# Block products with seven multiplications for the up projection of three chunk pairs

## The reference, cut to what matters

```python
D_MODEL = 1024
SEQ = 1024
DEPTH = 2
D_FF = 4 * D_MODEL
for l in range(DEPTH):
    ...
    x = layer_norm(DEEPNORM_ALPHA * x + jnp.einsum('btm,md->btd', mix, w_out[l]), ln_g[l, 0], ln_b[l, 0])
    hid = jnp.square(jax.nn.relu(jnp.einsum('btd,df->btf', x, w_up[l])))
    x = layer_norm(DEEPNORM_ALPHA * x + jnp.einsum('btf,fd->btd', hid, w_down[l]), ln_g[l, 1], ln_b[l, 1])
```

## Time and profile before

| | |
|---|---|
| time, median of 3 runs | 2765.5 us |
| span of the profiled execution | 2765.6 us |
| instructions | 36226 |
| PE busy | 2688.9 us, 12768 matmuls |
| DVE busy | 1645.8 us, 3330 |
| ACT busy | 998.6 us, 2055 |
| POOL busy | 1262.5 us, 1170 |
| DMA | 203.21 MB, mean 73 GB/s |
| mean granted TensorE clock | 0.990 |

### The profile page before, as it was taken

One profiled execution on the slowest core, in us unless ns is written; L12 is line 12 of the kernel. 1 busy time (PEld: TensorE's weight loads), 2 busy tenths in 40 slices (PEclk: granted clock), 3 DMA queues, 4 the chain that ended last, 5 costly groups with the idle time before them and its releaser, 6 DMA issues.

```text
span 2765.6 us, 36226 instructions
## 1 busy us (share of the span) xinstructions
PE 2688.9 (97%) x12768; PEld 2102.4 (76%) x12768; DVE 1645.8 (60%) x3330; ACT 998.6 (36%) x2055; POOL 1262.5 (46%) x1170
## 2 busy tenths in 40 slices
PE   8999899999999999999999998999999999999997
PEld 7788467668788888888887875676787888888886
DVE  3787876635534355544959877776364534355448
ACT  2476454442222212222435654443422222212223
POOL 5433700014666556666364346001156566566661
PEclk9999899999999999999999999999999999999999
DMA  5311344523311111101152122355323101111102
GB/s 155 89 46 46 68 91 93 131 105 97 122 33 32 61 62 61 50 17 63 65 138 57 44 74 57 79 109 119 114 89 111 57 27 39 61 62 61 50 20 80
DMA packets 97418, 203.21 MB, mean 73 GB/s; under 512 B 14010, under 2 KB 23162, under 8 KB 96954
## 3 DMA queue, kind: packets, MB, share of 16 engines
q1 hardware_dynamic: 87800, 175.58, 23.5%
q10 hardware_dynamic: 9440, 25.33, 2.5%
HBM read 138.04 MB, written 8.61 MB: 53 GB/s over the span
## 4 chain that ended last, share of the span: by engine, by line
PE 87%; DVE 7%; issue 2%; DMA 2%; ACT 1%; SPq 1%; POOL 0%; ACTq 0%; DVEq 0%; POOLq 0%
PE ps L1276 8%; PE ps L1278 8%; PE ps L1277 8%; PE ps L1158 8%; PE ps L1301 7%; PE ps L1300 7%; PE ps L1302 7%; PE ps L942 4%; PE ps L943 4%; PE ps L944 4%; PE ps L1206 2%; PE ps L1208 2%; PE ps L1207 2%; PE ps L1133 1%; PE ps L1100 1%
## 5 line engine op out<-in xcount | busy, mean ns | idle before, releaser
L900 POOL TENSOR_TENSOR wlo<-wraw,whi 128x512 fp32r<-128x512 f32 (+2 forms) x336 | 444.7, 1324 | 202.1 <-ACT whi L1363 180.2
L898 POOL CAST whi<-wraw 128x512 fp32r<-128x512 f32 (+2 forms) x272 | 183.6, 675 | 740.2 <-DMA wraw<-in_w_out 289.4
L1276 PE MATMUL ps<-xhi,whi 128*128 128x512 f32 x1024 | 406.1, 397 | 0.0
L1278 PE MATMUL ps<-xhi,wlo 128*128 128x512 f32 x1024 | 405.9, 396 | 0.0
L1277 PE MATMUL ps<-xlo,whi 128*128 128x512 f32 x1024 | 405.9, 396 | 0.0
L2064 DVE TENSOR_TENSOR common<-common,ps 128x512 f32<-128x512 f32 x104 | 69.6, 687 | 460.4 <-PE ps L1302 459.9
L1301 PE MATMUL ps<-wlo,op_hi 128*128 128x512 f32 x784 | 311.7, 398 | 0.0
L1300 PE MATMUL ps<-whi,op_hi 128*128 128x512 f32 x784 | 309.5, 395 | 0.0
L1302 PE MATMUL ps<-whi,op_lo 128*128 128x512 f32 x784 | 308.0, 393 | 0.0
L1507 ACT ACTIVATE probT<-ps 128x512 f32<-128x512 f32 (+2 forms) x456 | 205.2, 457 | 240.4 <-PE ps L1142 73.8
L900 POOL TENSOR_TENSOR wlo<-down_raw,whi 128x512 fp32r<-128x512 f32 x168 | 226.2, 1349 | 98.7 <-ACT whi L1363 92.0
(11 more groups left out here) (249 smaller groups left out, 5495.4 us busy)
## 6 DMA issues: line engine op xcount, KB each, us to landing
wraw<-in_w_up SPq DMA_DIRECT2D x144, 256.0 KB, 3.1
down_raw<-in_w_down SPq DMA_DIRECT2D x112, 256.0 KB, 3.6
wraw<-in_w_in SPq DMA_DIRECT2D x80, 256.0 KB, 2.7
slot<-q_part SPq DMA_DIRECT2D x72, 256.0 KB
slot<-k_part SPq DMA_DIRECT2D x72, 256.0 KB
wraw<-in_w_out SPq DMA_DIRECT2D x64, 256.0 KB, 2.8
slot<-q_part SPq DMA_DIRECT2D x48, 128.0 KB
slot<-k_part SPq DMA_DIRECT2D x48, 128.0 KB
```

The lines of the kernel that those rows point to most:

```text
L900: nc.gpsimd.tensor_tensor(lo, loaded, hi.bitcast(F32), ALU.subtract).then_inc(S["w_lo"], 1)
L1276: mm(ps[:, b, :], wh, xhi[:, k, tok], start=(k == 0), stop=False)
L1278: last = mm(ps[:, b, :], wl, xhi[:, k, tok], start=False, stop=(k == KT - 1))
```

## The change: three chunk pairs with seven products each

Chunks 0 and 1 are computed as before. Chunks 2 and 3, 4 and 5, 6 and 7 become pairs g = 1, 2, 3. For a pair, a 1024 x 1024 block of w_up stands against the 1024 x 1024 matrix x, both cut into quarters, and the same seven-product scheme is used (UPS names the weight side, UP_X the side of x). Each product has 4 slabs of 12 matmuls. Raw quarters of w_up lie in four "blocks" of four slabs; POOL forms S1 to S4 in place (line 1197 of the new kernel), right behind the lo part of a slab. The sums T1 to T4 of x are made once per layer while up(1) runs: POOL adds hi and lo of x back together (`whole`), DVE subtracts and makes lo parts, ACT makes hi parts, SyncE writes them to DRAM (x_sums, 8 MB per layer). In every pair they are loaded again, 1 MB at a time, into the three places that the operands of the down products use too. PSUM banks are drained by ACT copies and DVE additions (`add_product`).

The down products of two chunks now stand side by side and accumulate in the same banks, so that DVE adds 28 banks per pair instead of 28 per chunk; DOWNS gives (0,1), (2,3), (4,5) and (6). All hi parts of the slabs of pairs and of products are written by ACT. Semaphores that both layers can share are shared.

```diff
+DOWNS = [(0, 1), (2, 3), (4, 5), (6,)]
+N_DOWNS = len(DOWNS)
+PAIRS = range(1, N_DOWNS)
+UPS = ("A11", "A12", "S2", "S1", "S3", "S4", "A22")
+UP_X = ((0, 0), (4, 0), "T2", "T1", "T3", (4, 1), "T4")
+UP_BANK = (4, 0, 4, 0, 4, 0, 4)
+UP_FRESH = (0, 1, 3)
+X_SUMS = ("T1", "T3", "T2", "T4")
...
+def entries(g):
+    return [(q, c) for q in range(N_PROD) for c in DOWNS[g]]
...
+    for g in range(N_DOWNS):
+        if g:
+            for j, name in enumerate(UP_X):
+                if isinstance(name, str):
+                    for half in range(2):
+                        yield "x", g, (j, half)
+        for q, c in entries(g):
+            yield "operand", c, q
...
-    for c in range(FF_CHUNKS):
-        if c < LAST:
-            for k in range(KT):
-                yield "up", k, c + 1
-            for q in range(N_PROD):
-                for i in range(2):
-                    yield "product", i, (c, q)
+    for k in range(KT):
+        yield "up", k, 1
+    for g in range(N_DOWNS):
+        if g:
+            for j in range(len(UPS)):
+                for k in range(4):
+                    yield "pair", k, (g, j)
+        for q, c in entries(g):
+            for i in range(2):
+                yield "product", i, (c, q)
...
-    n for n, z in enumerate(SLABS) if z[0] == "product" and z[2][1] >= 4] + list(range(SLAB_LAST, N_SLABS))
+    n for n, z in enumerate(SLABS) if z[0] in ("product", "pair") or n in UP_SPLIT] + list(range(SLAB_LAST, N_SLABS))
...
+def sums_after(n):
+    kind, k, z = SLABS[n]
+    if kind == "up" and z == 1 and k >= 4:
+        return [("T3" if k % 2 == 0 else "T1", 0, (k - 4) // 2)]
+    if kind == "pair":
+        g, j = z
+        return {0: [("S1", g, k)], 1: [("S3", g, k)] + [("S2", g, 0)] * (k == 3), 2: [("S2", g, k + 1)] * (k < 3),
+                3: [("S4", g, k)], 4: [("T3" if k < 2 else "T1", DOWNS[g][0], k % 2)]}.get(j, [])
+    if kind == "product":
+        c, q = z
+        g = [c in cs for cs in DOWNS].index(True)
+        if len(DOWNS[g]) == 1:
+            return {1: [("T2", c, k)], 2: [("T4", c, k)]}.get(q, [])
+        odd = DOWNS[g][1]
+        if c != odd:
+            return {0: [("T2", c, k)], 1: [("T3", odd, k)], 2: [("T4", c, k)], 3: [("T4", odd, k)]}.get(q, [])
+        return {1: [("T1", c, k)], 2: [("T2", c, k)]}.get(q, [])
+    return []
...
+RECON_AFTER = {SLAB_UP0 + KT + 5: (0, 0), SLAB_UP0 + KT + 6: (0, 1), SLAB_UP0 + KT + 7: (1, 0), slab_up(1): (1, 1),
+               slab_up(1) + 3: (2, 0), slab_up(1) + 4: (2, 1), slab_up(1) + 5: (3, 0), slab_up(1) + 6: (3, 1)}
...
+                for g in PAIRS:
+                    split_done(slab_product(DOWNS[g - 1][-1], N_PROD - 1) + 1)
+                    load_block_of(g, "A21")
+                    load_block_of(g, "first A22")
+                    for k in range(8):
+                        load_down(DOWNS[g][0], k)
+                    load_x(g, t2, 0)
+                    load_x(g, t2, 1)
+                    load_x(g, t1, 0)
+                    load_x(g, t1, 1)
+                    load_x(g, t3_, 0)
+                    split_done(slab_pair(g, t2) + 3)
+                    sp.wait_ge(S["a_sum"], passed(l, "a_sum") + sum_count(("S4", g, 3)))
+                    load_block_of(g, "A22")
+                    more = g + 1 < N_DOWNS
+                    if more:
+                        split_done(slab_pair(g, UPS.index("S1")) + 3)
+                        load_block_of(g + 1, "A11")
+                    load_x(g, t3_, 1)
+                    load_x(g, t4, 0)
+                    if more:
+                        split_done(slab_pair(g, UPS.index("S3")) + 3)
+                        load_block_of(g + 1, "A12")
+                    load_x(g, t4, 1)
+                    split_done(slab_pair(g, UPS.index("S4")) + 3)
+                    if more:
+                        load_block_of(g, "low odd")
+                        split_done(slab_pair(g, UPS.index("A22")) + 3)
+                        load_block_of(g, "high odd")
...
+                nc.gpsimd.tensor_tensor(dst, a, b, op).then_inc(S["a_sum"], 1)
+                pool.wait_ge(S["a_sum"], passed(l, "a_sum") + sum_count(key))
...
+                for j in range(2 * half, 2 * half + 2):
+                    k_tile, tok = ((k, 0), (k, W), (4 + k, W), (4 + k, 0))[j]
+                    hi, lo = (z[:, k_tile, tok:tok + W].bitcast(F32) for z in (xhi, xlo))
+                    nc.gpsimd.tensor_tensor(xt[k % 2][j][:], hi, lo, ALU.add).then_inc(S["x_whole"], 1)
...
+                if n in RECON_AFTER:
+                    whole(*RECON_AFTER[n])
+                if sums_after(n):
                     pool.wait_ge(S["w_lo"], n + 1)
-                    t_sum(z[0], "T2" if z[1] == 1 else "T4", k)
+                for key in sums_after(n):
+                    difference(key)
...
+            def up_pair(g):
+                for j in range(len(UPS)):
+                    for k in range(4):
+                        n = slab_pair(g, j) + k
+                        z = ring(l, n)
+                        pe.wait_ge(S["w_lo"], n + 1)
+                        if isinstance(UP_X[j], str):
+                            place = place_of("x", g, (j, k // 2))
+                            if k % 2 == 0:
+                                pe.wait_ge(place_loaded[place], 16 * (l * X_LOADS[place] + x_loads(g, j, k // 2)))
+                            x_hi, x_lo = (part[place][:, k % 2] for part in (op_hi, op_lo))
+                        else:
+                            k_tile, half = UP_X[j]
+                            x_hi, x_lo = (part[:, k_tile + k, W * half:W * half + W] for part in (xhi, xlo))
+                        more = j not in UP_FRESH
+                        for f in range(4):
+                            if k == 0:
+                                up_bank_free(g, j, f)
+                            o = ps[:, UP_BANK[j] + f, :]
+                            wh, wl = whi[z][:, P * f:P * f + P], wlo[z][:, P * f:P * f + P]
+                            mm(o, wh, x_hi, start=(k == 0 and not more), stop=False, skip_group_check=more)
+                            mm(o, wh, x_lo, start=False, stop=False, skip_group_check=more)
+                            last = mm(o, wl, x_hi, start=False, stop=(k == 3), skip_group_check=more)
+                            if k == 3:
+                                last.then_inc(S["u_ready"], 1)
+                        if k < 3:
+                            last.then_inc(S["w_used"], 1)
...
+                    for c in cs:
+                        for i in range(2):
+                            n = slab_product(c, q) + i
+                            j = ring(l, n)
...
+            def x_differences(k):
+                t, low, high = xt[k % 2], xt_low[k % 2], xt_high[k % 2]
+                dve.wait_ge(S["x_whole"], passed(l, "x_whole") + 4 * k + 4)
+                for j, (a, b) in enumerate(((1, 0), (2, 1), (2, 0), (3, 2))):
+                    v_.tensor_tensor(t[j][:], t[a][:], t[b][:], ALU.subtract).then_inc(S["xt_sum"], 1)
+                    dve.wait_ge(S["xt_sum"], passed(l, "xt_sum") + 4 * k + j + 1)
+                for j in range(4):
+                    dve.wait_ge(S["xt_hi"], passed(l, "xt_hi") + 4 * k + j + 1)
+                    v_.tensor_tensor(low[j][:], t[j][:], high[j][:].bitcast(F32), ALU.subtract).then_inc(S["xt_lo"], 1)
+            def add_product(g, n, j, copy, c, half):
+                for f in range(4):
+                    dve.wait_ge(S["u_copy"], passed(l, "u_copy") + 12 * (g - 1) + 4 * copy + f + 1)
+                    dve.wait_ge(S["u_ready"], u_count(g, j) + f + 1)
+                    z = hidden[c % 2][:, f, W * half:W * half + W]
+                    v_.tensor_tensor(z, z, ps[:, UP_BANK[j] + f, :], ALU.add).then_inc(S["c_sum"], 1)
 
...
+            def down_sums(g):
+                todo, cs = entries(g), DOWNS[g]
+                for m, (q, c) in enumerate(todo):
+                    if c == cs[-1]:
+                        sum_product(g, q)
+                        dve.wait_ge(S["d_sum"], SUMS * g + 4 * q + 4)
+                    if m + PLACES < len(todo):
+                        next_q, next_c = todo[m + PLACES]
+                        operand_lo(next_c, next_q)
+                        if next_q == 2:
+                            s_sum(next_c, 2)
+                            s_sum(next_c, 3)
+                    if g == N_DOWNS - 1 and q == 4:
                         last_low(0)
...
+            for g in PAIRS:
+                even, odd = 2 * g, 2 * g + 1
+                add_product(g, 0, 1, 0, even, 0)
+                add_product(g, 1, 4, 2, odd, 1)
+                operand_lo(even, 0)
+                add_product(g, 2, 5, 1, even, 1)
+                s_sum(even, 0)
+                s_sum(even, 1)
+                if len(DOWNS[g]) > 1:
+                    operand_lo(odd, 0)
+                    operand_lo(even, 1)
+                    s_sum(odd, 0)
+                    s_sum(odd, 1)
+                else:
```

(65 more changed lines are left out.)

495 lines of the change are left out of this document (355 added, 140 removed).

## The result

The changed kernel takes 2845.5 us (median of four runs, 2838.9 to 2847.8) against 2766.3 before: ratio 1.028 [1.0267, 1.0292], slower. The forecast was 2802, range 2728 to 2842. The sign was right, the size was not: 79 us instead of 36. The profiled execution has a span of 2843.2 us, 77.6 more than before.

The account below looks back on a forecast made before the run. PE was taken to bound the MLPs, without holes. 2765.6 us less 67.4 for removed matmuls plus 103.6 of new waits (51.8 per layer) gave 2801.8; range 2728 to 2842, the forecast's own 2775 to 2828.

Parts of the forecast that it names:

- Base: MLPs of both layers: 288 matmuls fewer at 0.234 us each, 67.4 us less.
- D: Start of the down products: DVE and POOL take turns of 1.70 us, so PE waits 33 us per layer.
- F: Rival at the down products: DVE and POOL hardly meet, 1.11 us per DVE operation, 2732 us in all; chance 0.24.
- G: Rival at the down products: DVE and POOL block each other fully, 1.98 us per pair of operations, 2846 us; chance 0.12.
- B: S2 in the up pairs: POOL's slabs come slower than PE needs them, 3 us per pair, 9 per layer.
- A: Sums of x made during up(1): added POOL, DVE and ACT work costs PE 3 us per layer.
- E: Chunk 6 alone: its 8 sums and 4 lo parts come ahead of the first addition, 2 us per layer.
- C: Second half of T3: its load stands behind 8 slab loads on SyncE, 4.8 us per layer.
- rival I: PE's granted clock falls to 0.50 after waits, adding 12 to 24 us: 2814 to 2826; no separate chance given.

Follow-up runs that it names:

- the last version: Changed kernel with late S2/S4 sums, earlier T3 second half, reordered POOL S1/S2, plus chunk 6's S2 earlier and up(1) x additions one slab later: 2731.4 us, ratio 0.9869.
- fifth experiment: Changed kernel with POOL's differences T1, T2 and T4 of the down weights made on one column only, output incomplete: 2770.9 us, ratio 1.0011.
- the first: Changed kernel with DVE's sums S2 and S4 of the hidden blocks made two and three operands later in the down products: 2785.1 us, ratio 1.0064.
- the experiment that took most of it away: Changed kernel with 228 matmuls by a block of zeros added just ahead of PE's long waits: 2815.8 us, ratio 1.0178.
- three moves of order: Changed kernel with late S2/S4 sums on DVE, T3's second half loaded ahead of A22's reload, and POOL's S1 later, S2 earlier: 2739.0 us, ratio 0.9899.
- fourth experiment: Changed kernel with only POOL's order in the up pairs changed, S1 later and S2 earlier: 2805.7 us, ratio 1.0134.

## Why the prediction was wrong

**Base, right.** 288 matmuls fewer, 0.234 us each. With most of the waits taken out, the last version keeps half of the 67.4.

**D, right in mechanism, place and size.** 58.7 against 66. The turns of 1.70 are in the rows, the waits stand at the (odd, third) and (even, fourth) operand, 2.1 and 7.0 us where 4.5 and 6.5 were forecast. Both rivals on DVE's pace are out: F (1.11 per operation) and G (1.98). G's total, 2846, is the time that was measured, but by coincidence: it had 102 us for D in both layers and nothing for the clock. The fifth experiment shows the cause, the first the remedy.

**B and A, right**, 21.1 and 7.6 for 18 and 6. **E** was twice the forecast (8.6 for 4).

**C, right in place and chain, too small.** 16.9 for 9.6. In all six pairs POOL finished the last S4 0.6 us before PE began the slab ahead of T3, as reckoned ("about as PE begins that slab"). What was off is the time from the first load of the reload to the arrival of T3's second half, forecast at 11.2 us: in the four pairs with a next A11 it took 13.2, 12.2, 13.1 and 11.9. The third pair has 1 MB less in the queue, was reckoned to need no wait, and took 10.0, which cost PE 1.1. Why the loads took longer was not tested. The forecast also has a slip here: 11.2 less 8.4 is 2.8, not 2.4, so by its own terms C is 5.6 per layer and the sum 2803.4. Lastly, C hangs on the same small lead of POOL as B, which is why one move ended both.

**The waits as a whole** came out at 112.9 for 103.6, by misses on both sides: D was 7 too high, C 7, E 5, B 3 and A 2 too low.

**The step that failed is the clock.** The prediction had seen, named it as rival I with 12 to 24 us, and left it out of the sum, at 0. It measured 31, 25 in the experiment that took most of it away. The forecast's own range, 2775 to 2828, was said to count I, but its number did not. With I's middle, 18, in the sum the forecast would have been 2820, and the whole range moved up by as much would have ended at 2860. Without the clock the measured waits give 2811, 9 above the forecast. It was also undercounted: I looked for it at D's pauses only. In the MLPs the clock fell 15 times, and also behind C (4.2 and 3.3 us), E (4.3) and A (2.8). A cost that follows from the others' own numbers is a term, not a rival: with pauses of 4.5 and 6.5 us in the sum and the earlier trace rows on the page, the chance that the clock held at 1.00 was small.

The Trainium skill, TensorE: Matmul & The Clock Gate, section HAM oscillation — how this bites in real kernels, describes the pattern: a wait for data between blocks of matmuls lets the clock fall, and every next block starts slow. This trace agrees (0.50 at 1020 to 1025, behind each of the long D waits); the prediction did not draw on it.

## What to carry to other kernels

Price a pause of PE twice: once for the wait, start to start, and once for the matmuls behind it that run at the lower clock (here 31 us for 15 falls, some 2 us each; where four short waits of 0.6 to 1.5 us made up 3.2, the clock stayed at 1.00). When an engine is late, look first at what stands ahead of the late instruction and isn't needed yet: three moves of order, without any work taken away, were worth 106 us. And take away one wait before pricing the cure of several: two of them may hang on the same lead, as B and C did.

## What the runs showed of the hardware

- Matmuls by a block of zeros that add nothing to a bank kept the granted clock up: 1.00 in 995 to 1020 with 26 of them in it, where the same stage without them was at 0.89.
- The fall does not follow from a pause's length alone (lengths start to start). Behind a pause of 2.11 us in layer 1 of the fourth experiment's kernel (1170.3 us) the clock fell. It stayed at 1.00 behind 2.10 us in the changed kernel (1010.7), behind 2.80 in its layer 2 (2240.0), behind 2.94 at the last product of the last version, and behind 3.02 in layer 1 of the fifth experiment's kernel (835.6).
- Two engines with both inputs in SBUF and no gaps: 1.70 us per turn for a DVE operation of 0.69 and a POOL operation of 1.30 alone. The Trainium skill, SBUF — State Buffer, section SBUF: two separate sides, has the shared ports held by whichever starts first for its whole instruction, which would give an estimated 1.98 per turn; these rows show 1.70.
